# A hybrid decoder layer: gates and branch projections with tokens on partitions, the merged sum transposed for the output projection

## The chip, the cores and the metric

The kernel runs on one core of one Trainium2 chip. The metric is the time of one execution on the device, in microseconds (us). The engines: TensorE (PE in the rows, PEld its weight loads), VectorE (DVE), ScalarE (ACT), GpSimd (POOL), and SyncE (SP), which here only issues DMAs.

## The reference, cut to what matters

One layer on x of 256 tokens by 1024 channels, float32:

```
h = RMSNorm(x);  P = h @ w_in            # columns: rwkv 1792, attention 1536, pool 512, gates 3 x 1024
y0 = RWKV-7 time mixing (8 heads x 64), y1 = causal attention with ALiBi (8 x 64), y2 = pooling (4 x 128)
branch[n] = y[n] @ w_branch[n]           # 512 -> 1024 channels each, n = 0, 1, 2
x = x + (sum over n of sigmoid(P_gate[n]) * branch[n]) @ w_out
x = x + relu(RMSNorm(x) @ w_ff1)^2 @ w_ff2      # 1024 -> 4096 -> 1024
```

## The kernel before, in words

Every large product is done as three matmuls of rounded parts: a value is split into a high part and a remainder (w_hi and w_lo for weights, h_hi/h_lo, y_hi/y_lo, r_hi/r_lo for activations), and `mm3` (lines 460 to 463) adds high x high, high x low and low x high in one PSUM bank.

The weights pass through in 69 slots, the list `UNITS` (lines 59 to 69), 1 MB each, in two pieces of 128x1024. For each piece SyncE issues a DMA into `stage` (3 buffers, lines 433 to 436), ScalarE casts it to w_hi (line 823, "high") and VectorE subtracts to w_lo (line 1047, "low"), both into rings of 6 (`RING`). `split_places` sets the order: in slot t both engines prepare pieces 2t + 5 and 2t + 6. TensorE raises `used` after each half slot, and that frees ring places.

A slot has four quarters, p = 0 to 3; `part(t, p)` issues its dense matmuls, and `extra(t, p)` after it the small work of the mixers that is laid between. TensorE, ScalarE and VectorE walk the same (t, p) in program order: in a slot, ScalarE and VectorE do the first piece, extra 0, the second piece, extra 1, extra 2, `finish(t)` (what drains the slot's own result), extra 3.

The slots: 0 to 10 rwkv and attention columns, 11 and 12 the attention values, 13 and 14 pool columns, 15 to 26 the gates (`S_GATE` = 15), 27 to 32 the branches n = 1, 2, 0, each in two channel halves (`S_BR` = 27), 33 to 36 the output projection (`S_OUT` = 33), 37 to 68 the MLP.

There are two forms of a slot. In "feat" (and the branches before), 128x128 blocks of the weights are the stationary operand and the 256 tokens move: 48 matmuls of 256 columns, result with channels on partitions. In "tok" (slots 11 and 12, the output projection, and the second MLP product), a 128-token block of the activations is stationary and 512 weight columns move: 24 matmuls of 512 columns, result with tokens on partitions. A tok product of 1024 channels deep takes two slots for one 128x512 result per token half tt.

PSUM has 8 banks. `plan_turns` (lines 108 to 145) gives each result a bank; names without a fixed bank take 4 to 7 in turn (the ring), in the order in which TensorE comes to them. `room` makes TensorE wait until all earlier results of that bank are drained; `take` makes a reader wait until a result is there; `copied` waits for its drain. Before the change, feat slots use banks 0 and 1 in turn, attention scores bank 2, the transposed probabilities "pt" and the products "pv" bank 3, branches 0/1 and 2/3 in turn.

The mixers around the change: attention heads 0 to 7 run over slots 13 to 21 (score and pt after quarter 1, pv after quarter 3); the second half of the RWKV chunk work starts with "prod" (1, g, kind, e) over slots 17 and 18, which VectorE masks and copies (lines 1153 to 1165), goes on over slots 19 to 24, and ends with apply and group norm in 25 to 28.

Gates: ScalarE writes tanh(x/2) of each gate slot to `gates` (line 993). Branches: VectorE computes (tanh + 1) x branch (line 1298), GpSimd adds branches 1 and 2 (line 1428), VectorE adds branch 0 (line 1305), ScalarE writes y_hi = 0.5 x sum (line 999) and VectorE y_lo (line 1309). This sum has channels on partitions, as the output projection needs it for its stationary operand; TensorE waits there for `m_ready`.

## Time and profile before

| | us |
|---|---|
| median of 3 runs | 511.68 (510.59 to 511.97) |
| the profiled execution, whole | 510.58 |
| its span, first to last instruction | 508.8 |
| VectorE busy in it | 308.6 |
| ScalarE busy in it | 242.7 |
| GpSimd busy in it | 45.6 |

The mean granted clock of TensorE is 0.999. The span is what the timeline's microseconds count in; it starts at 0. Busy times of engines overlap, so they don't add up to it. The page's TensorE rows give each matmul from its start to its modelled end, and consecutive ones overlap: what one costs in a dense stretch is read from start to start.

### The profile page before, as it was taken

The page shows a single profiled execution, that of the slowest core. Times are in us where ns is not written, and L with a number is a line of the kernel's source. Part 1 is how long each engine was busy: PE and PEld are TensorE (multiplying, and loading weights), DVE is VectorE, ACT ScalarE, POOL GpSimd, SP SyncE. Part 2 cuts the span into 40 slices and gives each one's busy share as a digit, 9 for nine tenths or more (in the row PEclk, how much of TensorE's full clock was granted, in tenths as well). Part 3 has the DMA queues.
Part 4 walks back from the last instruction along what each step waited for, and adds up shares of the span by engine and source line. Part 5 has one row for each costly group of instructions (what it writes and reads, how often), then busy time and mean ns, then how long its engine had stood idle before and what let it go on. Part 6 is the DMA issues. An engine that isn't in the chain of part 4 may idle for free.

```text
span 508.8 us, 9618 instructions
## 1 busy us (share of the span) xinstructions
PE 494.9 (97%) x4064; PEld 451.0 (89%) x4064; DVE 308.6 (61%) x447; ACT 242.7 (48%) x365; POOL 45.6 (9%) x48
## 2 busy tenths in 40 slices
PE   3999999999999989999999999999999999999997
PEld 3989998988889778899999998899999999999995
DVE  4656898744463897446427986676555655555542
ACT  5676552454653236555333335655444544545440
POOL 1002003220660120000001220000000000000000
PEclk9999999999999999999999999999999999999999
DMA  9975462444422213454225557367666665665612
GB/s 262 270 210 160 133 172 78 126 124 125 126 84 83 84 55 112 126 140 131 84 84 170 177 166 194 124 203 222 195 183 191 187 186 173 200 197 180 200 44 82
DMA packets 101660, 76.87 MB, mean 151 GB/s; under 512 B 2545, under 2 KB 93297, under 8 KB 101618
## 3 DMA queue, kind: packets, MB, share of 16 engines
q1 hardware_dynamic: 101618, 76.26, 50.6%
q8 instruction: 32, 0.52, 0.4%
q14 instruction: 10, 0.08, 0.1%
HBM read 75.20 MB, written 1.05 MB: 150 GB/s over the span
## 4 chain that ended last, share of the span: by engine, by line
PE 93%; DVE 4%; ACT 1%; DMA 1%; issue 1%; POOL 0%; ACTq 0%; POOLq 0%
PE bank L461 26%; PE bank L462 25%; PE bank L463 25%; PE bank L691 1%; PE bank L669 1%; PE bank L707 1%; PE bank L554 1%; DMA xs<-in_x 1%; PE bank L785 1%; DVE mat L1157 1%; PE bank L742 1%; PE bank L731 1%; PE bank L741 1%; PE bank L723 1%; PE bank L635 1%
## 5 line engine op out<-in xcount | busy, mean ns | idle before, releaser
L1047 DVE TENSOR_TENSOR w_lo<-stage,w_hi 128x1024 fp32r<-128x1024 f32 x138 | 171.6, 1249 | 121.1 <-ACT w_hi L823 121.0
L823 ACT CAST w_hi<-stage 128x1024 fp32r<-128x1024 f32 x138 | 143.7, 1048 | 117.8 <-PE bank L463 90.4
L461 PE MATMUL bank<-h_hi,w_hi 128*128 128x256 f32 x656 | 193.0, 294 | 0.9 <-DVE h_lo L1071 0.7
L462 PE MATMUL bank<-h_lo,w_hi 128*128 128x256 f32 x656 | 186.4, 284 | 0.0
L463 PE MATMUL bank<-h_hi,w_lo 128*128 128x256 f32 x656 | 186.2, 284 | 0.0
L461 PEld LDWEIGHTS bank<-h_hi,w_hi 128*128 128x128 f32 x656 | 126.3, 193 | 9.7 <-issue 6.8
L462 PEld LDWEIGHTS bank<-h_lo,w_hi 128*128 128x128 f32 x656 | 126.6, 193 | 0.6
L463 PEld LDWEIGHTS bank<-h_hi,w_lo 128*128 128x128 f32 x656 | 126.4, 193 | 0.0
L461 PE MATMUL bank<-w_hi,r_hi 128*128 128x512 f32 x128 | 50.0, 391 | 0.0
L462 PE MATMUL bank<-w_lo,r_hi 128*128 128x512 f32 x128 | 50.0, 390 | 0.0
L463 PE MATMUL bank<-w_hi,r_lo 128*128 128x512 f32 x128 | 49.8, 389 | 0.0
L1363 POOL TENSOR_TENSOR small<-small 128x8 f32<-128x8 f32 (+2 forms) x9 | 14.1, 1568 | 170.4 <-DVE small L1215 104.7
L463 PEld LDWEIGHTS bank<-w_hi,r_lo 128*128 128x128 f32 x128 | 24.0, 188 | 5.1
L461 PEld LDWEIGHTS bank<-w_hi,r_hi 128*128 128x128 f32 x128 | 24.1, 188 | 4.6
L462 PEld LDWEIGHTS bank<-w_lo,r_hi 128*128 128x128 f32 x128 | 24.1, 188 | 4.4
L1012 ACT ACTIVATE mat<-bank 128x512 f32<-128x512 f32 x16 | 9.6, 598 | 28.0 <-PE bank L463 27.9
L1321 DVE TENSOR_TENSOR mat<-mat 128x512 f32<-128x512 f32 x16 | 11.1, 691 | 19.2 <-ACT mat L1012 19.2
L461 PE MATMUL bank<-y_hi,w_hi 128*128 128x256 f32 x64 | 18.2, 284 | 0.0
L463 PE MATMUL bank<-y_hi,w_lo 128*128 128x256 f32 x64 | 18.1, 283 | 0.0
L462 PE MATMUL bank<-y_lo,w_hi 128*128 128x256 f32 x64 | 18.1, 283 | 0.0
L940 ACT ACTIVATE att<-att,small 128x128 f32<-128x128 f32 (+1 forms) x16 | 7.2, 448 | 21.4 <-DVE small L1246 21.4
L461 PE MATMUL bank<-w_hi,y_hi 128*128 128x512 f32 x32 | 12.5, 392 | 0.0
(210 smaller groups left out, 613.7 us busy)
## 6 DMA issues: line engine op xcount, KB each, us to landing
stage<-in_w_ff SPq DMA_DIRECT2D x64, 512.0 KB, 4.3
stage<-in_w_in SPq DMA_DIRECT2D x54, 512.0 KB, 3.9
stage<-in_w_branch SPq DMA_DIRECT2D x12, 512.0 KB, 3.6
stage<-in_w_out SPq DMA_DIRECT2D x8, 512.0 KB, 3.4
xs<-in_x SPq DMA_DIRECT2D x2, 512.0 KB, 4.4
out<-xs SPq DMA_DIRECT2D x4, 256.0 KB, 2.1
cst<-in_consts SPq DMA_DIRECT2D x1, 897.0 KB, 7.4
lora<-in_g_up SPq DMA_DIRECT2D x1, 256.0 KB
```

The costliest lines, as they stand in the source:

```text
L461: pe.matmul(o, lh, rh, start=first, stop=False)
L462: pe.matmul(o, lh, rl, start=False, stop=False)
L463: return pe.matmul(o, ll, rh, start=False, stop=last)
L554: ins = pe.matmul(o[:, 256 * i:256 * i + 256], bk[c][rows, kind, j], ar[c][rows, j], start=True, stop=True)
L635: ins = pe.matmul(o[:, 4 * c + 2 * jj:4 * c + 2 * jj + 2], sq_att[n % 2][:, T * jj + P * c:T * jj + P * c + P], cst[:, C_BLK:C_BLK + P:HD] ...
L669: ins = pe.matmul(both[b][to, HD * j:HD * j + HD], gm[rows, 2 * j + e, 0, rows], x_c[rows, 2 * j + e], start=True, stop=True)
L823: nc.scalar.copy(w_hi[:, v % RING], stage[:, v % STAGES]).then_inc(hi_done, 1)
L940: nc.scalar.activation(w, w, ACT.Exp, bias=nmax[:, tt:tt + 1], accum_out=psm[:, tt:tt + 1]).then_inc(exps_ready, 1)
L1012: nc.scalar.activation(ffs[i % 2], o[:], ACT.Relu).then_inc(drained_of(("ff", i)), 1)
L1047: dve.tensor_tensor(w_lo[:, v % RING], stage[:, v % STAGES], w_hi[:, v % RING].bitcast(F32), ALU.subtract)\
L1321: link(dve.tensor_tensor(fsq[i % 2], ffs[i % 2], ffs[i % 2], ALU.mult))
L1363: pool.tensor_tensor(ap, ap, half.to_broadcast(shape), ALU.pow).then_inc(done, 1)
```

## The change

The gates become tok slots: six groups of 512 columns, each two slots (depth halves) long, in banks (2g + tt) mod 3; the tanh of both token halves comes at the end of the second slot. The branch slots become tok slots too, half a depth per piece, tokens on partitions; VectorE's multiply-add and addition go by token half. Scores move to bank 3; pt, pv and the pool products move into the ring of banks 4 to 7. The merged sum now has tokens on partitions and goes through four groups of four transposes ("mt", `turned_place`) in slots 32 and 33; ScalarE and VectorE write y_hi and y_lo from their PSUM result. The arithmetic is the same.

```diff
@@ -60,7 +60,8 @@
 UNITS += [("feat", N_RWKV + N_ATTN + c) for c in (0, 256)]
-UNITS += [("feat", N_RWKV + N_ATTN + N_POOL + 256 * q) for q in range(12)]
+GATES_AT = N_RWKV + N_ATTN + N_POOL
+UNITS += [("tok", GATES_AT + 512 * g, kh) for g in range(6) for kh in range(2)]
@@ -125,12 +126,16 @@
                     use(("unit", t), t % 2, dense=True)
+                elif u[0] == "tok" and u[2] == 0 and u[1] >= GATES_AT:
+                    g = (u[1] - GATES_AT) // 512
+                    for tt in range(TT):
+                        use(("tok", u[1], tt), (2 * g + tt) % 3, dense=tt == 1)
...
                     b = 2 * ((t - S_BR + 1) % 2)
-                    use(("unit", t, 0), b, dense=True)
+                    use(("unit", t, 0), b)
@@ -143,6 +148,11 @@
     return turn
+
+
+def turned_place(t, p):
+
+    return {(S_OUT - 1, 1): (0, 0), (S_OUT - 1, 2): (0, 1), (S_OUT, 1): (1, 0), (S_OUT, 3): (1, 1)}.get((t, p))
@@ -197,13 +207,15 @@
         if p == 1 and h >= 1:
-            out += [(("pt", h - 1), 3)]
+            out += [(("pt", h - 1),)]
         if p == 1 and h < HEADS:
-            out += [(("score", h), 2)]
+            out += [(("score", h), 3)]
         if p == 3 and h >= 1:
-            out += [(("pv", h - 1), 3)]
+            out += [(("pv", h - 1),)]
     if t == S_PY and p in (0, 2):
-        out += [(("pool", p // 2), 2 + p // 2)]
+        out += [(("pool", p // 2),)]
+    if turned_place(t, p):
+        out += [(("mt", *turned_place(t, p)),)]
@@ -216,8 +228,8 @@
         for tt in range(TT):
-            if u[0] == "branch":
-                ends[("unit", t, tt)] = 2 * t + 1 + tt
+            if u[0] == "branch" and tt == 1:
+                ends[("unit", t, 1)] = 2 * t + 2
@@ -385,7 +397,7 @@
         pad_ready, pool_step, pd_ready, yp_hi = (sem(n) for n in ("pad_ready", "pool_step", "pd_ready", "yp_hi"))
@@ -394,7 +406,7 @@
             kind = UNITS[v // 2][0]
-            k = {"feat": KD, "ff1": KD, "ff2": 1, "branch": W // P}.get(kind, 2)
+            k = {"feat": KD, "ff1": KD, "ff2": 1}.get(kind, 2)
@@ -408,9 +420,8 @@
             if u[0] == "branch":
-                c = 512 * u[2] + 256 * half
-                return w_branch[0, u[1], :, c:c + 256].rearrange("(k p) n -> p k n", p=P)
-            if u[0] == "tok":
+                r, m, c = 256 * half, w_branch[0, u[1]], 512 * u[2]
+            elif u[0] == "tok":
@@ -503,12 +514,15 @@
                             pe.wait_ge(yr_ready, TT)
-                    rh, rl, k0 = {1: (y_hi, y_lo, 0), 2: (y_hi, y_lo, 4), 0: (r_hi, r_lo, 0)}[u[1]]
-                    name = ("unit", t, p // 2)
-                    o = ps(name) if i else room(pe, name)
-                    for k in range(W // P):
-                        ins = mm3(o[:, T * i:T * i + T], wh[:, k, P * i:P * i + P], wl[:, k, P * i:P * i + P],
-                                  rh[:, k0 + k], rl[:, k0 + k], k == 0, k == W // P - 1)
+                    lh, ll, k0 = {1: (y_hi, y_lo, 0), 2: (y_hi, y_lo, 4), 0: (r_hi, r_lo, 0)}[u[1]]
+                    name = ("unit", t, i)
+                    o = room(pe, name) if p < 2 else ps(name)
+                    for kk in range(2):
+                        k = 2 * (p // 2) + kk
+                        ins = mm3(o[:], lh[:, k0 + k, P * i:P * i + P], ll[:, k0 + k, P * i:P * i + P],
+                                  wh[:, kk], wl[:, kk], k == 0, k == 3)
+                    if p == 2:
+                        ins.then_inc(full_of(name), 1)
@@ -516,8 +530,8 @@
                         first, last = u[1] == 0, u[1] == 1
-                        if i == 0:
-                            pe.wait_ge(m_ready, 2 * u[1] + p // 2 + 1)
+                        if p < 2:
+                            copied(pe, ("mt", u[1], i))
@@ -795,6 +809,13 @@
                     ins.then_inc(full_of(("pool", i)), 1)
+                if turned_place(t, p):
+                    ch, tt = turned_place(t, p)
+                    pe.wait_ge(m_pre, 2 * ch + tt + 1)
+                    o = room(pe, ("mt", ch, tt))
+                    for k in range(4):
+                        ins = pe.transpose(o[:, P * k:P * k + P], gates[ch][:, tt, P * k:P * k + P], ident)
+                    ins.then_inc(full_of(("mt", ch, tt)), 1)
@@ -951,6 +972,11 @@
                     ins.then_inc(yp_hi, 1)
+                if turned_place(t, p):
+                    ch, tt = turned_place(t, p)
+                    o = take(act, ("mt", ch, tt))
+                    nc.scalar.mul(y_hi[:, 4 * ch:4 * ch + 4, P * tt:P * tt + P], o[:].rearrange("p (k t) -> p k t", k=4), 0.5)\
+                      .then_inc(m_hi, 1)
@@ -983,21 +1009,18 @@
                     nc.scalar.activation(sq_att[n % 2], o[:], ACT.Square).then_inc(drained_of(("unit", t)), 1)
+                elif S_GATE <= t < S_BR:
+                    if u[2] == 1:
+                        for tt in range(TT):
+                            name = ("tok", u[1], tt)
+                            o = take(act, name)
+                            nc.scalar.activation(gates[(t - S_GATE) // 2][:, tt], o[:], ACT.Tanh, scale=0.5)\
+                              .then_inc(drained_of(name), 1)
...
                         nc.scalar.copy(vatt[:, tt], o[:]).then_inc(drained_of(name), 1)
-                elif S_GATE <= t < S_BR:
-                    o = take(act, ("unit", t))
-                    nc.scalar.activation(gates[(t - S_GATE) // 2][:, t % 2 ^ S_GATE % 2], o[:], ACT.Tanh, scale=0.5)\
-                      .then_inc(drained_of(("unit", t)), 1)
-                elif u[0] == "branch" and u[1] == 0:
-                    for i in range(2):
-                        m = 2 * u[2] + i
-                        act.wait_ge(m_pre, m + 1)
-                        nc.scalar.mul(y_hi[:, 2 * m:2 * m + 2], gates[u[2]][:, i].rearrange("p (k t) -> p k t", k=2), 0.5)\
-                          .then_inc(m_hi, 1)
@@ -1265,6 +1288,14 @@
                     ins.then_inc(drained_of(("pool", i)), 1)
+                if turned_place(t, p):
+                    ch, tt = turned_place(t, p)
+                    dve.wait_ge(m_hi, 2 * ch + tt + 1)
+                    o = take(dve, ("mt", ch, tt))
+                    part = y_hi[:, 4 * ch:4 * ch + 4, P * tt:P * tt + P].bitcast(F32)
+                    dve.scalar_tensor_tensor(out=y_lo[:, 4 * ch:4 * ch + 4, P * tt:P * tt + P], in1=part, scalar=0.5,
+                                             in0=o[:].rearrange("p (k t) -> p k t", k=4), op0=ALU.mult, op1=ALU.subtract)\
+                       .then_inc(drained_of(("mt", ch, tt)), 1)
@@ -1292,23 +1323,16 @@
                     g = 2 * n + ch
-                    for i in range(2):
-                        copied(dve, ("unit", S_GATE + 2 * g + i))
-                        o = take(dve, ("unit", t, i))
-                        dve.scalar_tensor_tensor(out=gates[g][:, i], in0=gates[g][:, i], scalar=1.0, in1=o[:],
+                    for tt in range(TT):
+                        copied(dve, ("tok", GATES_AT + 512 * g, tt))
+                        o = take(dve, ("unit", t, tt))
+                        dve.scalar_tensor_tensor(out=gates[g][:, tt], in0=gates[g][:, tt], scalar=1.0, in1=o[:],
                                                  op0=ALU.add, op1=ALU.mult)\
-                           .then_inc(drained_of(("unit", t, i)), 1)
-                    if n == 0:
-                        dve.wait_ge(sum_ready, ch + 1)
-                        for i in range(2):
-                            copied(dve, ("unit", t, i))
-                            dve.tensor_tensor(gates[ch][:, i], gates[ch][:, i], gates[2 + ch][:, i], ALU.add).then_inc(m_pre, 1)
-                        for i in range(2):
-                            m = 2 * ch + i
-                            dve.wait_ge(m_hi, m + 1)
-                            dve.scalar_tensor_tensor(out=y_lo[:, 2 * m:2 * m + 2], scalar=0.5, op0=ALU.mult, op1=ALU.subtract,
-                                                     in0=gates[ch][:, i].rearrange("p (k t) -> p k t", k=2),
-                                                     in1=y_hi[:, 2 * m:2 * m + 2].bitcast(F32)).then_inc(m_ready, 1)
+                           .then_inc(drained_of(("unit", t, tt)), 1)
+                        if n == 0:
+                            dve.wait_ge(sum_ready, ch + 1)
+                            copied(dve, ("unit", t, tt))
+                            dve.tensor_tensor(gates[ch][:, tt], gates[ch][:, tt], gates[2 + ch][:, tt], ALU.add).then_inc(m_pre, 1)
```

## Rows read from the trace of the kernel before

**Rows 1.** The page: busy time of each engine, and the engines of the chain.

```profile
PE 494.9 (97%) x4064; PEld 451.0 (89%) x4064; DVE 308.6 (61%) x447; ACT 242.7 (48%) x365; POOL 45.6 (9%) x48
...
PE 93%; DVE 4%; ACT 1%; DMA 1%; issue 1%; POOL 0%; ACTq 0%; POOLq 0%
```

**Rows 2.** Windows, slots 27 to 32: length, then PE, PEld, DVE, ACT, POOL busy, clock, DMA, GB/s.

```profile
266.20:301.20 35.00, 35.00 (x294) 35.00 (x294) 29.17 (x36) 14.80 (x17) 7.79 (x3) 1.00 0.54 167
```

**Rows 3.** Timeline of PE, slot 18: start, us, engine, line, out<-in, count [idle before <-releaser].

```profile
185.24 0.52 PE L769 MATMUL bank<-cst,att 128*128 128x128 f32 x3 [2.00 <-DVE y_lo L1051]
```

**Rows 4.** Timeline of PE: first matmul of slots 27, 28, 33 and 34.

```profile
266.16 0.28 PE L461 MATMUL bank<-y_hi,w_hi 128*128 128x256 f32 x1
...
271.92 0.28 PE L461 MATMUL bank<-y_hi,w_hi 128*128 128x256 f32 x1
...
301.15 0.40 PE L461 MATMUL bank<-w_hi,y_hi 128*128 128x512 f32 x1
...
306.62 0.39 PE L461 MATMUL bank<-w_hi,y_hi 128*128 128x512 f32 x1
```

**Rows 5.** Timeline of POOL, ACT and DVE, slot 31 and the start of slot 32.

```profile
291.97 3.23 POOL L1428 TENSOR_TENSOR big<-big 128x1024 f32<-128x1024 f32 x1 [2.45 <-DVE big L1298]
...
292.76 1.05 ACT L823 CAST w_hi<-stage 128x1024 fp32r<-128x1024 f32 x1 [1.83 <-PE bank L463]
...
293.85 2.44 DVE L1047 TENSOR_TENSOR w_lo<-stage,w_hi 128x1024 fp32r<-128x1024 f32 x1 [0.91 <-ACT w_hi L823]
296.21 1.27 DVE L1298 SCALAR_TENSOR_TENSOR big<-big,bank 128x512 f32<-128x512 f32 x2
297.41 1.28 DVE L1305 TENSOR_TENSOR big<-big 128x512 f32<-128x512 f32 x2
```

**Rows 6.** Timeline of PE: first quarter of slots 10 and 11, and what follows it.

```profile
94.01 0.36 PE L461 MATMUL bank<-h_hi,w_hi 128*128 128x256 f32 x1
...
95.61 0.50 PE L669 MATMUL bank<-mat 64*64 64x64 f32 x17
...
102.71 0.47 PE L461 MATMUL bank<-w_hi,h_hi 128*128 128x512 f32 x1
...
104.27 0.69 PE L669 MATMUL bank<-mat 64*64 64x64 f32 x32
```

**Rows 7.** Timeline of PE, slot 12: four transposes and the two matmuls after them.

```profile
115.71 0.60 PE L645 MATMUL bank<-cst,att 128*128 128x128 f32 x4
116.06 0.48 PE L461 MATMUL bank<-w_hi,h_hi 128*128 128x512 f32 x1
116.38 0.39 PE L462 MATMUL bank<-w_lo,h_hi 128*128 128x512 f32 x1
```

**Rows 8.** Timeline of DVE, slots 17 and 18.

```profile
181.80 0.67 DVE L1157 TENSOR_TENSOR mat<-bank,cst 128x512 f32<-128x512 f32 x1
...
185.12 1.23 DVE L1047 TENSOR_TENSOR w_lo<-stage,w_hi 128x1024 fp32r<-128x1024 f32 x1
186.38 1.29 DVE L1157 TENSOR_TENSOR mat<-bank,cst 128x512 f32<-128x512 f32 x2
```

**Rows 9.** Timeline of ACT, slot 26.

```profile
260.60 0.60 ACT L993 ACTIVATE big<-bank 128x512 f32<-128x512 f32 x1 [0.85 <-PE bank L463]
...
264.95 0.63 ACT L926 ACTIVATE lmix<-lora 128x512 f32<-128x512 f32 x1 [2.82 <-DVE lora L1211]
265.49 1.03 ACT L823 CAST w_hi<-stage 128x1024 fp32r<-128x1024 f32 x1
266.43 0.59 ACT L993 ACTIVATE big<-bank 128x512 f32<-128x512 f32 x1
```

**Rows 10.** Timeline of ACT and PE, end of slot 14 and start of slot 15.

```profile
137.93 0.59 ACT L1005 COPY ops<-bank 128x512 f32<-128x512 f32 x1
...
138.57 0.39 PE L461 MATMUL bank<-h_hi,w_hi 128*128 128x256 f32 x1
```

More of the change, by code:

```diff
@@ L387, in build_layer @@
         pad_ready, pool_step, pd_ready, yp_hi = (sem(n) for n in ("pad_ready", "pool_step", "pd_ready", "yp_hi"))
-        sum_ready, m_pre, m_hi, m_ready = (sem(n) for n in ("sum_ready", "m_pre", "m_hi", "m_ready"))
+        sum_ready, m_pre, m_hi = (sem(n) for n in ("sum_ready", "m_pre", "m_hi"))
         ss2_ready, h2_hi = sem("ss2_ready"), sem("h2_hi")
```

## The prediction

> **What bounds the kernel now.** I read the chain of work that ended last first: 93% of it is TensorE, which is busy for 97% of the span [rows 1]. The reader is to see that a microsecond off TensorE's queue is a microsecond off the span, and that any new wait of TensorE is one on. Then the windows. In the branch stage (slots 27 to 32, 266.2 to 301.2 us) TensorE is busy for all 35.0 us, VectorE for 29.2 and ScalarE for 14.8, with DMA at 0.54 [rows 2], so VectorE is second, with little to spare. The one wait of TensorE inside the changed stages is the 2.0 us at 185.24, for VectorE [rows 3]. Each slot brings 1 MB of weights in both forms, cast and subtracted two to three slots ahead: the w_lo instruction at 293.85 makes the first piece of slot 34, which TensorE touches at 306.62 [rows 4, 5]. Supply is therefore not what I look at. The question is the order of TensorE's queue and its banks.
>
> **The gain: half as many matmuls, each twice as wide.** A slot in the old form is 48 matmuls of 256 columns, in the new form 24 of 512. The columns streamed are the same. With nothing between, a slot of 48 takes 271.92 - 266.16 = 5.76 us (0.120 each) and a slot of 24 takes 306.62 - 301.15 = 5.47 us (0.228 each) [rows 4]; that slot's first quarter is slower because it follows 256-wide work, the others take 1.36 us, so a bare quarter (p = 0 to 3) goes from 1.44 to 1.36: 0.08 us saved. Where other matmuls stand around a quarter, less is left: with the same neighbours before and after, the 256-wide quarter takes 95.61 - 94.01 = 1.60 us and the 512-wide one 104.27 - 102.71 = 1.56 [rows 6]: 0.04 saved.
> I count quarters by what the code puts before them. Slots 15 and 16: 8 with neighbours, 0.32 us. Slots 17 and the first half of 18: 6, which earn nothing, since TensorE then waits for VectorE anyway [rows 3]. From there to slot 25: 24 with neighbours and 6 bare, 0.96 + 0.48 = 1.44. Slots 26 to 32: 28 bare, 2.24, less 0.04 at the two re-entries. Together 0.32 + 1.44 + 2.20 = 4.0 us. Ends: 3.0 (0.05 in every bare quarter, if the slower pitch stays) and 4.8 (0.08 in every quarter that counts, with slots 17 and 18).
>
> The Trainium skill, TensorE: Matmul & The Clock Gate, section Back-to-back issue gap, gives the gap between isolated matmuls as N/2.4 + 2.5 ns, a fixed part of 2.5 ns where the rows above hold some 13 ns at either width. By that page of the Trainium skill, an estimate, the 432 matmuls that go would bring 432 x 2.5 ns = 1.1 us and the sum below would be 2.9 us worse. The rows are of this very form in this kernel, so they decide.
>
> **The transposes.** The merged sum now has tokens on partitions and must be turned: 16 transposes of 128x128 f32 in four groups, at (slot 32, after p = 1 and p = 2) and (slot 33, after p = 1 and p = 3), all in TensorE's queue. The same shape in groups of four stands between 512-wide quarters in slot 12: 116.06 - 115.71 = 0.35 us, and the first matmul after it takes 0.32 instead of 0.23 [rows 7]. With the slower pitch of the quarter behind (0.03) that is 0.46 a group, 1.85 us for four. Ends 1.4 (without re-entry) and 2.2. ScalarE's four multiplications and VectorE's four subtractions for y_hi and y_lo were there before at the same size (128x512), now read from PSUM; they cost nothing by themselves, since neither engine is the bound, but they move in their queues, which is a term below.
>
> **New wait 1: the shared ring (slot 18).** The gates take banks 0 to 2, so pt and pv go from bank 3 into the ring of banks 4 to 7. Following the uses: pt of head 4, after p = 1 of slot 18, gets the bank of product (1,1,kind 1,e 0), issued after p = 0 of that slot. VectorE is a phase behind there: it drains the kind-0 products at 181.80, then the pv remainder, then a w_lo at 185.12, and only then the kind-1 products from 186.38, the first of two done at about 187.0 [rows 8]. Before, pt waited only for the pv remainder and went at 185.24 [rows 3]. Now it goes at about 187.15: 1.9 us on. Two earlier waits of the ring (some 0.8 us for product (1,0,kind 2,e 1), 0.6 us for (1,1,kind 1,e 1)) and the last kind-2 product's wait for pv fall inside this one. Behind pt in the queue stand score 5, the rest of slot 18 and everything after; VectorE needs score 5 only after the pair at 186.38 and one more w_lo (188.8), so it isn't pushed on and the loss isn't doubled. Ends: 0 (the old wait only) and 2.5 (both kind-1 products drained first). I take 1.9, straight from the row.
>
> **New wait 2: bank 2 at slot 27.** Branch unit (27, tt 0) takes bank 2, whose last user is the second token half of gate 5; it is complete only when slot 26 ends. TensorE reaches slot 27 at 260.39 + 5.44 = 265.83 in old time (slot 26 started one slot before 266.16, less its 0.08 a quarter) and must wait for the tanh. ScalarE's order there is tanh, w_hi, square, w_hi, tanh [rows 9]. The first tanh (slot 25) goes, since only every second gate slot drains now, so w_hi, the group norm's chain through VectorE and the square come 0.5 earlier; the w_hi of 265.49 starts at about 265.0, the two tanh follow at 265.95 and 266.45 and end at 267.05. TensorE starts at 267.15: 1.3 us. Ends 0.6 (one tanh after the slot's end) and 1.9 (nothing moves up: the two from 266.43). Before, the bank of the next slot was always free a slot earlier.
>
> **Other banks.** Gate 0 takes bank 0 at slot 15, that of unit 14: its copy runs 137.93 to 138.52 and TensorE arrives at 138.57 [rows 10], so it costs 0 to 0.2; I take 0. In the other gates the third bank gives a quarter and the extras as cover, about 1.5 us against one 0.6 us tanh that can start a quarter before the slot's end: 0, at worst 0.5.
>
> **New wait 3: VectorE between the merge and the output projection.** In slot 31 VectorE ends its second w_lo late, at 296.3, because of the GpSimd addition beside it; the two multiply-adds and two additions then run to 298.7 [rows 5]. In old time the new slot 31 starts 0.2 earlier; the first transposes wait until the first addition (297.4) and TensorE comes at 297.6, so 0 there. But VectorE then has two w_lo (to 301.0) before the first y_lo of the transposed block, done at 301.65, and the output projection (slot 33) is reached at 301.2: 0.5 us, with the semaphore. The second block's y_lo (302.3) is before its use (303.2). Slot 34 and later have a slot's room. Ends 0 and 1.9 (one more w_lo plus its wait ahead of it).
>
> **The sum.** -4.0 + 1.85 + 1.9 + 1.3 + 0.5 = +1.55, taken as +1.6 us. The MLP (slots 37 on) isn't touched and keeps its pace. The profiled execution took 510.6 us, of which 508.8 are its span; so 510.4 span and 512.2 for a profiled execution. The median of the runs shown, 511.68, is 1.1 above the profiled one; the difference is put on the median: 513.3 us. 0.3%, here 1.5 us, is about what can be told from no change; the forecast lies at that edge.
>
> **Rivals.**
> Faster. The covers hold after all: pt's and bank 2's waits are short, because VectorE and ScalarE run ahead once TensorE pauses. For it: in slots 19 to 26 TensorE never waits. Against: both waits follow from instructions that stand in program order with rows for each. Price: -4.0 + 1.85 = -2.15, so 509.5; it decides below 510.1, where at most 0.6 of the three waits may be left. 12%.
> Much slower. VectorE becomes the bound around slots 28 to 36: 29.2 of 35.0 us busy already [rows 2], slots shorter by 0.3 each, and a chain addition, transposes, w_lo, y_lo at the projection's start. If each of the four transposed blocks is met one w_lo (1.23) late, not one block 0.5 late, +4.4 more at most, about +2.5 likely: 515.8. Against: the w_lo run far ahead. 15%.
> The 512-wide form gives less than in the MLP: the pitch of 0.232 of slots 11 and 12 and of the first quarter of slot 33 stays. Gain 3.0 instead of 4.0: 514.3. By the gap that the Trainium skill states there the same mechanism, pushed to its end, gives 516.2. 13%, nearly all of it on the former, as [rows 4] speak against it.
> The forecast, with its own spread of about 1 us: 60%.
>
> **How the numbers follow.** Slower by over 0.3% (above 513.2): half of the forecast's 60, most of the third and all of the second rival: 0.53. Faster (below 510.1): 0.10. Same: 0.37. Range 511.0 to 515.8: below it most of the first rival, above it the tail of the second; about 2 in 10.
>
> **What would show it.** On TensorE: 18 slots of 24 wide matmuls, a bare one of 5.44 to 5.47 us; groups of four transposes at 0.35; idle before pt (head 4) of about 3 to 4 us in all over slots 17 and 18, where it was 2.0, released by the kind-1 product's copy; about 1.3 idle ahead of slot 27 released by the tanh; half a microsecond ahead of slot 33 released by y_lo. If the waits are there and the span still falls, the wide quarters gave more than 0.08 and 0.04. If TensorE waits in slots 28 to 36 for w_lo or y_lo beyond 1 us, the second rival holds.

## The result, and the profile after

The changed kernel takes 515.20 us, the median of four runs (514.51 to 515.66); the kernel before took 511.83 beside it (510.59 to 512.04). The ratio is 1.0076, with a 95% interval of 1.0056 to 1.0096: slower, inside the range forecast, and 1.9 us above the 513.3 that was forecast. The change itself costs 3.4 us, where 1.6 were forecast. The profiled execution took 515.11 us, 513.3 of them its span, with a mean granted clock of TensorE of 0.993; before, it was 510.58, 508.8 and 0.999.

The page of the changed kernel: TensorE still bounds it, with 416 fewer matmuls (432 go, 16 transposes come), yet more busy time than in [rows 1]. The row of PEclk, the granted clock in 40 slices, has a 7 in it.

```profile
PE 498.4 (97%) x3648; PEld 429.9 (84%) x3648; DVE 309.3 (60%) x447; ACT 242.6 (47%) x365; POOL 45.6 (9%) x48
...
PEclk9999999999999979999999999999999999999999
...
PE 91%; DVE 5%; ACT 1%; DMA 1%; issue 1%; SPq 0%; ACTq 0%
```

The longest waits of TensorE (line waited at, releaser: us in total, times, longest). The first is the start of the kernel. Then come pt of head 4 (L783) for the copy of a product, the branch stage for the tanh (L1017), and products (L571) for a copy; the 0.4 put down to "issue" is the one at slot 33.

```profile
PE bank L553 <- DVE big L1082: 6.9, 1, 6.9
PE bank L783 <- DVE mat L1180: 1.4, 1, 1.4
PE bank L472 <- ACT big L1017: 1.2, 1, 1.2
PE bank L472 <- DVE h_lo L1094: 0.7, 1, 0.7
PE bank L571 <- DVE mat L1180: 0.5, 1, 0.5
PE bank L472 <- issue: 0.4, 1, 0.4
```

The timeline of TensorE through slots 17 and 18, with lines left out between. Two waits stand in brackets. Two more hide in the durations: the eight matmuls at 179.80 take 2.00 us, where eight of the same kind take 1.14 at 176.34, and the eight at 183.33 take 1.49, where they took 0.72 to 0.79 in the kernel before. Together 0.54 + 0.86 + 0.75 + 1.36 = 3.5 us without work. Behind it a wide matmul starts every 0.43 us (191.16 to 191.58), and no longer every 0.23.

```profile
174.12 0.71 PE L571 MATMUL bank<-ops 64*128 64x128 f32 x4 [0.54 <-DVE mat L1180]
176.34 1.14 PE L568 MATMUL bank<-ops 64*128 64x256 f32 x8
...
179.80 2.00 PE L568 MATMUL bank<-ops 64*128 64x256 f32 x8
183.33 1.49 PE L571 MATMUL bank<-ops 64*128 64x128 f32 x8
186.18 0.74 PE L783 MATMUL bank<-cst,att 128*128 128x128 f32 x3 [1.36 <-DVE mat L1180]
...
191.16 0.63 PE L472 MATMUL bank<-w_hi,h_hi 128*128 128x512 f32 x1
191.58 0.63 PE L473 MATMUL bank<-w_lo,h_hi 128*128 128x512 f32 x1
```

The windows say why (columns as in [rows 2]; the column before the last two is the granted clock). From 186.1 to 193.0 TensorE is busy and its clock is 0.52, its lower level of 1.2 GHz; just behind, it is 1.00 again.

```profile
186.10:193.00 6.90, 6.82 (x18) 4.91 (x19) 5.66 (x16) 2.06 (x6) 1.09 (x1) 0.52 0.52 152
193.20:196.20 3.00, 3.00 (x28) 1.77 (x29) 0.81 (x2) 1.91 (x3) 0.00 (x0) 1.00 0.00 0
```

The price, piece by piece against the same pieces at 2.4 GHz (in the kernel of experiment 1 below): pt, the score and the way to the next quarter take 2.25 us instead of 1.30, and the two quarters behind, each with what follows it, 2.73 and 2.40 instead of 1.49 and 1.46; together 3.1 us. The forecast had no such term.

The timeline of TensorE at slot 27, in the branch stage, at a group of transposes and at slot 33: a wait of 1.20 for the tanh, bare wide matmuls whose w_hi step is 0.68 us (twice that, 1.36, is a quarter), and a wait of 0.45.

```profile
269.90 0.47 PE L472 MATMUL bank<-w_hi,y_hi 128*128 128x512 f32 x1 [1.20 <-ACT big L1017]
...
276.14 0.39 PE L472 MATMUL bank<-w_hi,y_hi 128*128 128x512 f32 x1
276.82 0.39 PE L472 MATMUL bank<-w_hi,y_hi 128*128 128x512 f32 x1
...
300.41 0.60 PE L817 MATMUL bank<-cst,big 128*128 128x128 f32 x4
300.77 0.48 PE L472 MATMUL bank<-w_hi,r_hi 128*128 128x512 f32 x1
...
304.67 0.47 PE L472 MATMUL bank<-w_hi,y_hi 128*128 128x512 f32 x1 [0.45 <-issue]
```

Laid on each other at the first weight matmul, the traces differ so, in us: wide form -3.8; slot 0, which the change doesn't touch, -0.2; waits of slots 17 and 18 +2.0; lower clock behind them +3.1; slot 27 +1.36; transposes, slot 33 and gate 0's bank +2.6. That is +5.1. The first weight matmul came 0.5 earlier after the change (11.25 against 11.79), by nothing that it does, which leaves the +4.5 of the spans.

### The profile page after: what moved, and what is told of

The parts are those of the page before. It is cut to its first block, busy times and chain, and to the rows that moved or that the text cites. A ratio compares the mean times of both kernels' runs of the same rounds, so it can differ in the third digit from the quotient of the medians.

```text
span 513.3 us, 8782 instructions
## 1 busy us (share of the span) xinstructions
PE 498.4 (97%) x3648; PEld 429.9 (84%) x3648; DVE 309.3 (60%) x447; ACT 242.6 (47%) x365; POOL 45.6 (9%) x48
## 4 chain that ended last, share of the span: by engine, by line
PE 91%; DVE 5%; ACT 1%; DMA 1%; issue 1%; SPq 0%; ACTq 0%
PE bank L472 26%; PE bank L474 24%; PE bank L473 24%; PE bank L705 1%; PE bank L683 1%; PE bank L721 1%; DMA stage<-in_w_in 1%; PE bank L568 1%; DVE mat L1180 1%; ACT w_hi L844 1%; DVE w_lo L1070 1%; PE bank L799 1%; PE bank L756 1%; PE bank L745 1%; PE bank L790 1%
## 5 line engine op out<-in xcount | busy, mean ns | idle before, releaser
L472 PE MATMUL bank<-h_hi,w_hi 128*128 128x256 f32 x464 | 135.0, 291 | 0.9 <-DVE h_lo L1094 0.7
L473 PE MATMUL bank<-h_lo,w_hi 128*128 128x256 f32 x464 | 132.3, 285 | 0.0
L474 PE MATMUL bank<-h_hi,w_lo 128*128 128x256 f32 x464 | 132.2, 285 | 0.0
L472 PEld LDWEIGHTS bank<-h_hi,w_hi 128*128 128x128 f32 x464 | 89.8, 194 | 5.0 <-issue 3.4
L473 PEld LDWEIGHTS bank<-h_lo,w_hi 128*128 128x128 f32 x464 | 89.9, 194 | 0.6
L474 PEld LDWEIGHTS bank<-h_hi,w_lo 128*128 128x128 f32 x464 | 89.8, 194 | 0.0
L472 PE MATMUL bank<-w_hi,h_hi 128*128 128x512 f32 x112 | 49.7, 443 | 0.0
L474 PE MATMUL bank<-w_hi,h_lo 128*128 128x512 f32 x112 | 44.8, 400 | 0.0
L473 PE MATMUL bank<-w_lo,h_hi 128*128 128x512 f32 x112 | 44.7, 400 | 0.0
L474 PE MATMUL bank<-w_hi,y_lo 128*128 128x512 f32 x64 | 25.0, 391 | 0.0
## 6 DMA issues: line engine op xcount, KB each, us to landing
stage<-in_w_ff SPq DMA_DIRECT2D x64, 512.0 KB, 4.1
stage<-in_w_in SPq DMA_DIRECT2D x54, 512.0 KB, 3.9
stage<-in_w_branch SPq DMA_DIRECT2D x12, 512.0 KB, 3.9
stage<-in_w_out SPq DMA_DIRECT2D x8, 512.0 KB, 4.6
xs<-in_x SPq DMA_DIRECT2D x2, 512.0 KB, 3.9
```

The costliest lines, as they stand in the source:

```text
L472: pe.matmul(o, lh, rh, start=first, stop=False)
L473: pe.matmul(o, lh, rl, start=False, stop=False)
L474: return pe.matmul(o, ll, rh, start=False, stop=last)
```

## The experiments

The kernel before ran beside each batch, on the same chip: 511.61 us (33 runs, 510.05 to 512.63) beside the first four, 511.45 (29 runs, 510.34 to 512.58) beside the next four, 511.53 (30 runs, 510.37 to 512.93) beside the last four. The ratios below are against these, with 95% intervals.

### 1. Work put into the idle time of slot 18

Theory: the idle time in slots 17 and 18 let the clock fall. So it is filled, with eight matmuls into bank 3 that nobody reads.

```diff
+                if (t, p) == (18, 1):
+                    o = room(pe, ("score", 5))
+                    for _ in range(8):
+                        pe.matmul(o[:], h_hi[:, 0, 0:P], h_hi[:, 0:2].rearrange("p k t -> p (k t)"), start=True, stop=True)
```

> The changed kernel, with eight extra 512-column matmuls of h_hi into bank 3 (the scores' bank, overwritten by score 5) after quarter 1 of slot 18, ahead of the kind-2 products: about 1.8 us of work in time in which TensorE otherwise waits for bank 5 and then for bank 6. Theory (the granted clock falls to half because TensorE was idle in slots 17 and 18): the clock stays full, pt of head 4 still starts when the kind-1 product is drained, and the kernel gains the 3.0 us that half speed costs: about 512.2 us. Rival (the wide form or chance lowers the clock there): the clock falls as before, 515.2 us, up to 515.7 if the extra matmuls push pt.

512.0 us (510.75 to 513.49), ratio 1.001 (0.9999 to 1.0022): eight matmuls more, and 3.2 us less than the changed kernel. Timeline and window of this kernel, the same stretch:

```profile
183.01 1.98 PE L665 MATMUL bank<-h_hi 128*128 128x512 f32 x8
184.92 0.72 PE L571 MATMUL bank<-ops 64*128 64x128 f32 x8
185.96 0.52 PE L787 MATMUL bank<-cst,att 128*128 128x128 f32 x3 [0.32 <-DVE mat L1184]
```

```profile
186.10:193.00 6.90, 6.90 (x53) 4.75 (x56) 5.87 (x17) 3.54 (x9) 1.09 (x1) 1.00 0.50 152
```

pt starts when it did, because VectorE is what it waits for (185.96, and 186.18 in the changed kernel), but what follows goes at full clock: 53 matmuls in the window, small ones among them, where there were 18. In all 12 runs the mean clock was 1.00. Without the idle time the clock didn't fall. In the traces the price is 3.1 us; by the medians it is 3.2 us, or 2.8 against the changed kernel's runs of experiment 12.

### 2. Slot 27's banks swapped

```diff
-                    b = 2 * ((t - S_BR + 1) % 2)
+                    b = 2 * ((t - S_BR) % 2)
...
-                        use(("out", u[2], tt), 2 * (1 - u[2]) + tt, dense=tt == 1)
+                        use(("out", u[2], tt), 2 * u[2] + tt, dense=tt == 1)
```

> The changed kernel with the branches' bank pairs swapped (slot 27 takes banks 0 and 1, slot 32 banks 2 and 3, the output projection's halves swapped to match). Theory (bank 2 alone makes TensorE wait at slot 27): no wait there, 1.3 us less, 513.9 us. Rival (TensorE meets a tanh anyway, at quarter 1 of slot 27 or at slot 28): less than 0.3 us gained, 515.0 or more.

514.58 us (511.42 to 514.79), ratio 1.0048 (1.0033 to 1.0064). The wait of slot 27 is gone, and TensorE stands 1.38 us at the first transposes instead. (The profiled execution had a mean clock of 0.997: the same waits in slots 17 and 18, but a stretch at half clock of only 3.4 us behind them.) Timeline of TensorE and of VectorE in this kernel:

```profile
298.48 0.66 PE L817 MATMUL bank<-cst,big 128*128 128x128 f32 x4 [1.38 <-DVE big L1335]
```

```profile
291.27 1.27 DVE L1329 SCALAR_TENSOR_TENSOR big<-big,bank 128x512 f32<-128x512 f32 x2
292.47 4.55 DVE L1070 TENSOR_TENSOR w_lo<-stage,w_hi 128x1024 fp32r<-128x1024 f32 x2
296.95 0.67 DVE L1329 SCALAR_TENSOR_TENSOR big<-big,bank 128x512 f32<-128x512 f32 x1
297.73 0.69 DVE L1335 TENSOR_TENSOR big<-big 128x512 f32<-128x512 f32 x1
```

VectorE's additions stand behind two w_lo that take 4.55 us together; a w_lo with nothing beside it takes 1.23 [rows 8], and from 292.71 to 295.93 GpSimd runs its addition. (By the Trainium skill, SBUF — State Buffer, section Who interferes with whom, a VectorE instruction with two SBUF inputs contends with a GpSimd instruction that reads SBUF; these rows agree.) So the gain was given back 30 us later, by neither of the two accounts: VectorE has no more room there than slot 27's wait had given it.

### 3. The kernel before, with the ring alone

Only the banks of pt, scores, pv and pool are changed, as the change has them; the 256-wide form stays.

```diff
-            out += [(("pt", h - 1), 3)]
+            out += [(("pt", h - 1),)]
...
-            out += [(("score", h), 2)]
+            out += [(("score", h), 3)]
...
-            out += [(("pv", h - 1), 3)]
+            out += [(("pv", h - 1),)]
...
-        out += [(("pool", p // 2), 2 + p // 2)]
+        out += [(("pool", p // 2),)]
```

> The kernel before, with one part of the change alone: scores in bank 3, pt, pv and the pool products in the ring of banks 4 to 7. Gates and branches keep their 256-column form, nothing is transposed. Theory (the shared ring brings the wait, and the idle time brings the lower clock): pt of head 4 starts 1.9 us later, and the clock falls to half for some 7 us, 3.0 us more: about 4.9 us over the kernel before. Rival (the wide form is needed for the fall): 1.9 us over the kernel before and the clock full.

512.84 us, ratio 1.0036 (1.0015 to 1.0057). The 12 runs spread over 510.84 to 515.69. Every run comes with its mean granted clock, and that sorts them: 1.00 in five (510.84 to 511.99, mean 511.4), 0.997 in two (512.8 and 512.9), 0.993 in five (513.90 to 515.69, mean 515.0). One program, and its groups lie 3.6 us apart. The profiled execution, 515.14 us, was one of the last group; its wait and its window are those of the changed kernel:

```profile
186.89 0.87 PE L769 MATMUL bank<-cst,att 128*128 128x128 f32 x3 [1.36 <-DVE mat L1157]
```

```profile
186.50:193.30 6.80, 6.41 (x26) 5.46 (x27) 5.98 (x17) 1.47 (x5) 1.09 (x1) 0.51 0.56 157
```

The fall needs no wide matmul. The ring alone brings it, but not in each execution, and so the median is neither the theory's +4.9 us nor the rival's +1.9. Whether an execution with clock 1.00 also waited less could not be seen, since one of the 12 was profiled; that the ring's own +1.7 to +2.0 us is missing from the mean of the five at 1.00 (511.4) speaks for it.

### 4. Gates in two banks, pt and pv kept in bank 3

```diff
-                        use(("tok", u[1], tt), (2 * g + tt) % 3, dense=tt == 1)
+                        use(("tok", u[1], tt), 1 - tt, dense=tt == 1)
...
...
-            out += [(("pt", h - 1),)]
+            out += [(("pt", h - 1), 3)]
-            out += [(("score", h), 3)]
+            out += [(("score", h), 2)]
-            out += [(("pv", h - 1),)]
+            out += [(("pv", h - 1), 3)]
...
-        out += [(("pool", p // 2),)]
+        out += [(("pool", p // 2), 2 + p // 2)]
```

> The changed kernel with the banks of before for everything but the gates: gates in banks 1 (first token half) and 0, scores in 2, pt and pv in 3, pool products in 2 and 3; so the next branch slot's bank 2 is free too. Theory: the ring's wait (1.9), the half clock (3.0) and the wait at slot 27 (1.3) all go, and two banks are enough for the gates since the first half's tanh starts a quarter before the slot's end: 6.2 us less than the changed kernel, about 509.0 us, faster than the kernel before by 1.5 to 3 us. Rival (two banks are too few: each of the five gate changes waits for a tanh, 0.5 to 0.8 us each): 512 us.

512.91 us (511.92 to 514.63), ratio 1.0033 (1.002 to 1.0045). That is 3.9 us over the theory's 509.0. pt's wait is back to the 2.00 of [rows 3], slot 27's is gone, but 1.02 us of waiting stand at the first transposes, as in experiment 2; the clock kept 1.00 in the profile. A new wait stands in slot 19. Timeline of TensorE, then of ScalarE:

```profile
192.08 0.47 PE L472 MATMUL bank<-w_hi,h_hi 128*128 128x512 f32 x1 [2.46 <-ACT big L1017]
```

```profile
190.47 0.40 ACT L961 ACTIVATE att<-att,small 128x128 f32<-128x128 f32 x1 [4.92 <-DVE small L1269]
...
191.37 1.06 ACT L1017 ACTIVATE big<-bank 128x512 f32<-128x512 f32 x2
```

The tanh that frees the bank stands behind the exponentials, and these wait 4.92 us for VectorE. The rival had small waits at every gate; it is one large one. The third bank is what hides the tanh there.

### 5 and 6. VectorE's split moved behind the products, without and with the swap

```diff
+                both = t in (17, 18)
-                for v in split_places(2 * t):
+                for v in () if both else split_places(2 * t):
...
-                for v in () if late else split_places(2 * t + 1):
+                for v in () if late or both else split_places(2 * t + 1):
...
-                for v in split_places(2 * t + 1) if late else ():
+                for v in (*split_places(2 * t), *split_places(2 * t + 1)) if both else split_places(2 * t + 1) if late else ():
```

> The changed kernel, where VectorE does its w_lo of slots 17 and 18 after extra 3 of the slot instead of between (same instructions, pieces needed two slots later). Theory (TensorE's waits in slots 17 and 18 stand behind VectorE's four w_lo there, 1.2 us each, one of them with a wait for w_hi; the half clock comes from those waits): the waits of the ring and also the wait of 2.0 us that the kernel before had go, the clock stays full; left over the kernel before are -4.2 (wide form) - 2.0 + 1.85 (transposes) + 1.35 (slot 27) + 0.6 (projection) = -2.4: about 509.2 us. Rival (VectorE's chain of products and softmax itself is too long): the waits of TensorE there are still over 2 us in all, 511 us or more.

> The kernel with deferred w_lo, and also the branches' bank pairs swapped, so that slot 27 doesn't wait for the tanh in bank 2. Theory (what slot 27 no longer waits, the transposes in slot 32 wait for VectorE's merge instead, as in the run with the swap alone): within 0.4 us of the run with the deferral alone. Rival (the wait at slot 32 came from the disturbed slot 18): 1.3 us less than it.

511.52 us (510.49 to 513.36), ratio 1.0003 (0.9989 to 1.0016), and with the swap 512.37 (510.88 to 512.98), ratio 1.001 (0.9997 to 1.0023). The first is 2.3 us over the theory's 509.2, and the rival's waits of over 2 us are there: pt still waits, now 2.50 us in one piece, because slot 17's own two w_lo (2.36 us) still stand ahead of the products:

```profile
181.92 2.36 DVE L1070 TENSOR_TENSOR w_lo<-stage,w_hi 128x1024 fp32r<-128x1024 f32 x2
184.31 1.29 DVE L1180 TENSOR_TENSOR mat<-bank,cst 128x512 f32<-128x512 f32 x2
```

But the scattered waits ahead of it are gone, and in this trace so is the fall behind it; the median is 3.7 us less than the changed kernel's for 1 us less of waiting. None of its 12 runs had a mean clock of 0.993. That isn't the whole story, though: the sixth kernel has the same code in slots 17 and 18 and the same single wait, and in its profiled execution the clock fell behind it. The wait and the window of the sixth, then the window of the fifth:

```profile
183.51 0.52 PE L783 MATMUL bank<-cst,att 128*128 128x128 f32 x3 [2.50 <-DVE mat L1180]
```

```profile
183.50:190.40 6.90, 6.89 (x19) 4.95 (x19) 4.45 (x15) 3.11 (x7) 1.09 (x1) 0.54 0.36 133
```

```profile
185.10:192.00 6.90, 6.85 (x41) 4.71 (x45) 5.78 (x17) 4.71 (x10) 1.10 (x1) 1.00 0.38 138
```

So one wait of 2.50 us can be followed by the fall, and four pieces aren't needed for it. What the deferral changed, in these runs, is how often it comes: a mean clock of 0.993 or less in 5 of the 36 runs of the fifth, sixth and seventh, against 8 of the 11 of the changed kernel (here and in experiment 12). The swap again took 1.35 off slot 27 and gave 1.4 to the transposes, as its theory had it.

### 7. The swap, with VectorE's late w_lo moved too

On top of the sixth: in slots 31 to 33 the second w_lo (and in 32 and 33 the second w_hi) goes behind the merge.

```diff
-                late = t == S_FF - 1
+                late = t in (S_OUT - 2, S_OUT - 1, S_OUT, S_FF - 1)
```

> As the run with deferral and swapped banks, and VectorE also does the second w_lo of slots 31, 32 and 33 after extra 3 (ScalarE the second w_hi of 32 and 33). Theory (the merge comes late because a w_lo, blocked by the GpSimd addition, stands ahead of it in slot 31, and two stand ahead of the first y_lo): TensorE's waits in slots 32 and 33 go, 1.9 us less than the run with deferral alone: about 507.3 us, faster than the kernel before by some 4 us. Rival (w_lo arrive too late for the slots after, or the merge waits for the branch result itself): 509 us or more.

510.10 us (508.34 to 514.01), ratio 0.9979 (0.9958 to 1.0001). The waits at slots 27, 32 and 33 are gone together: with room on VectorE the swap pays. It is 1.4 us less than the fifth, where 1.9 were expected, and 2.8 over the theory's 507.3, most of which is what the fifth was over its own. Its profiled execution also had half the clock behind pt's wait of 2.50 us, from 183.9 to 190.7.

### 8. The kernel before, with the split moved

> The kernel before, with the same deferral of VectorE's w_lo in slots 17 and 18 and nothing of the change. Theory: its one wait in that stage (2.0 us) goes, 509.6 us. Rival (the wait moves to another instruction): 511 us or more.

509.67 us (508.60 to 509.89), ratio 0.9956 (0.9939 to 0.9972). The time is the theory's 509.6, but the rival's mechanism is there too: the 2.0 us of [rows 3] are gone, and 1.63 stand later for ScalarE's copy:

```profile
188.73 0.62 PE L785 MATMUL bank<-att,big 128*64 128x256 f32 x2 [1.63 <-ACT att L935]
```

The mean clock was 0.999 or 1.00 in five of its six runs, where the kernel before had 0.997 in 74 of the 92 runs beside all batches. Between the profiled executions the gain is 0.9 us (spans of 507.9 and 508.8), between the medians 1.8; what makes the rest was not found.

### 9 to 11. The split of three pieces held until after slot 18

In slots 17 and 18 VectorE splits nothing but the first piece of slot 17; the three others are held to the end of slot 18. Alone, with the swap and the late w_lo of the seventh, and in the kernel before:

```diff
-                for v in split_places(2 * t):
+                for v in () if t == 18 else split_places(2 * t):
...
-                for v in () if late else split_places(2 * t + 1):
+                for v in () if late or t in (17, 18) else split_places(2 * t + 1):
...
-                for v in split_places(2 * t + 1) if late else ():
+                for v in range(40, 43) if t == 18 else split_places(2 * t + 1) if late else ():
```

> The changed kernel, where VectorE holds three w_lo (pieces 40, 41, 42) until after extra 3 of slot 18. In the deferral run the two w_lo of slot 17 still stood ahead of the kind-1 products in slot 18, and a w_hi waited for its DMA; here nothing of the kind stands there. Theory: the kind-1 product is drained within 0.5 us of when TensorE comes for its bank, no wait over 0.7 us before pt of head 4, and the clock stays full in all runs: 2.3 us less than the deferral run, about 509.2 us. Rival (VectorE's own work on products, softmax and group norm is what TensorE waits for): a wait of 2 us or more stays, 511 us.

> Held w_lo as in the run before, swapped bank pairs for the branches, and the second w_lo of slots 31, 32 and 33 after extra 3 (w_hi of 32 and 33 too). Theory: all waits that the change brought are gone but the transposes' own time: before - 4.2 (wide form) - 2.0 (its old wait) + 1.9 (transposes) + 0.2 = 4.1 us under the kernel before, about 507.3 us. Rival (the lower clock comes with any wait over 1 us somewhere in slots 17 to 19): some runs at 510 us, median over 508.5.

> The kernel before with the same three w_lo held. Theory: its wait of 2.0 us goes and no other takes its place: 509.4 us, so that the run with all repairs is 2 us below it (wide form 4.2, transposes 1.9). Rival (the wide form gives nothing once waits are gone): the two are equal.

Alone 511.94 us (509.45 to 512.97), ratio 1.0002 (0.9985 to 1.0019): no wait ahead of pt, and 2.24 us in slot 19: the theory's 509.2 is missed, and the rival's 2 us of waiting are there, though not for its reason. Timeline of TensorE and VectorE:

```profile
196.81 0.69 PE L705 MATMUL bank<-mat 64*64 64x64 f32 x32 [2.24 <-DVE mat L1206]
```

```profile
188.75 3.48 DVE L1070 TENSOR_TENSOR w_lo<-stage,w_hi 128x1024 fp32r<-128x1024 f32 x3
194.71 1.22 DVE L1070 TENSOR_TENSOR w_lo<-stage,w_hi 128x1024 fp32r<-128x1024 f32 x1 [2.48 <-ACT w_hi L844]
195.85 0.75 DVE L1206 TENSOR_TENSOR mat<-bank,cst 128x256 f32<-128x256 f32 x2
```

The wait was moved by a slot, not taken away: the product's copy stands behind w_lo there too. With swap and late w_lo it is 509.93 (507.22 to 511.82), ratio 0.9965 (0.9948 to 0.9982): the one version of the changed kernel that beats the kernel before, by 0.35%. The theory's 507.3 was reached by the run of 507.22 alone; the rival (a median over 508.5, by the clock) came. The four runs at a mean clock of 0.999 or 1.00 took 508.0 in the mean, the eight others 510.3. In the kernel before the same hold gives 511.62 (509.56 to 513.93), ratio 0.9996 (0.9979 to 1.0014), and not the 509.4 expected: here too a wait takes the old one's place in slot 19, with 3.4 us at half clock behind it.

```profile
196.67 0.69 PE L691 MATMUL bank<-mat 64*64 64x64 f32 x32 [2.56 <-DVE mat L1183]
```

It lies 1.7 above the tenth, where 2 were expected; the five runs at 1.00 (mean 510.0) lie 2.0 above the tenth's four. With much the same wait left in both, that is what wide form and transposes are worth, -4.0 + 1.85 in the forecast. The eighth, the kernel before with the split moved, is no slower than the tenth by its ratio.

### 12. The changed kernel once more

> The changed kernel as it is, beside the others. Theory (the clock falls in most executions but not in all, by where the idle time of slots 17 and 18 falls): median 514.5 to 515.2 us, a spread of some 3 us, the fastest near 512 us, which is the sum without the clock's 3.0. Rival: all within 1 us.

514.76 us (512.97 to 515.59), ratio 1.0053 (1.0033 to 1.0073). Five of the seven runs had a mean clock of 0.993 (mean 515.0 us); the two others, 0.997 and 1.00, took 513.0. Median and spread are the theory's; the fastest lie 1 us above its 512, so that the clock is worth 2.0 us between these groups.

## Why the prediction was right in direction and in the terms that it had, and 1.9 us low

Wide form, -4.0: measured -3.8. A bare quarter went from 1.44 to 1.36 us, one with neighbours lost some 0.04; from the start of slot 27 to that of slot 32 it is 1.4 us (27.79 against 29.23). The rows of slots 11, 12 and 33 carried over to the stages that took the form.

Transposes, +1.85: a group costs 0.36 to 0.38 and some 0.1 at the re-entry, as [rows 7] gave it.

Shared ring, +1.9: +2.0, which is how much longer pt starts after VectorE's copy of the kind-0 products (5.44 us, where it was 3.44). The 3 to 4 us of idle time over the two slots were 3.5.

Bank 2 at slot 27, +1.3: +1.36 from start to start, 1.20 of it shown as idle, released by the tanh. The order that the prediction gave ScalarE (w_hi, then both tanh) is the order of the trace:

```profile
267.75 1.03 ACT L844 CAST w_hi<-stage 128x1024 fp32r<-128x1024 f32 x1
268.69 1.07 ACT L1017 ACTIVATE big<-bank 128x512 f32<-128x512 f32 x2
```

Slot 33, +0.5: 0.45 shown idle, about 0.6 with the slower first matmul, right after y_lo; its two w_lo stood ahead as told:

```profile
301.61 2.36 DVE L1070 TENSOR_TENSOR w_lo<-stage,w_hi 128x1024 fp32r<-128x1024 f32 x2
303.88 1.28 DVE L1296 SCALAR_TENSOR_TENSOR y_lo<-bank,y_hi 128x512 fp32r<-128x512 f32 x2
```

Gate 0's bank, 0: 0.1. VectorE as the bound (the second rival) did not come; this window answers to [rows 2], with TensorE busy for 34.35 of 34.80 us (the 0.45 of slot 33 are missing), and VectorE at 84% of it:

```profile
270.40:305.20 34.80, 34.35 (x157) 28.07 (x156) 29.18 (x37) 14.39 (x16) 7.76 (x3) 1.00 0.57 175
```

What the prediction lacked stands in its first step: "any new wait of TensorE is one on". A wait can also decide at which clock the work behind it runs. pt's wait was priced at its length; the idle time of 3.5 us around it cost 3.1 us more behind it in the profiled execution. In the trace that makes the sum +1.55 + 3.1 = +4.7, against a span longer by 4.5. No rival held this: all three were about order and pitch, and the covers were judged at one clock. [rows 2] shows a clock of 1.00 and the text passed over it, since in that window nothing waits.

That only 1.9 us were missing in the end is luck. By its own sum the profiled execution should have taken 512.2 us; it took 515.1, 2.9 more. The prediction then added 1.1 us, because the kernel before had its median that far above its profiled execution. After the change that distance was 0.1 (515.11 and 515.20), so 1.0 of the 2.9 us were covered by a term that had nothing to do with them.

Why the kernel before had that distance stays open. The mean clock doesn't explain it: of its 92 later runs the six at 1.00 (mean 511.2) and the 74 at 0.997 (511.3) are alike, and only the eleven at 0.993 (512.5) are slower. In which slot its clock falls was not profiled.

## What to carry to other kernels

Where TensorE is the bound, price each of its waits twice: by its length, and by the clock of the work behind it. The second price comes only in a share of the executions, so take it from several runs and not from one profile. Count the waits that hide in long durations too. Compare the mean clock of the runs before reading a difference of under one per cent, and look into a profile for where the clock fell: the mean doesn't say it. Two waits on one second engine are one debt: freeing TensorE at slot 27 was paid at slot 32 until VectorE itself had less ahead of the merge.

## What was not expected of the hardware

The granted clock fell to half for 6.8 us after four pieces of idle time, none over 1.4 us, 3.5 us in all between 174 and 186. After one piece of 2.0 in the same place (the profiled kernel before), after one of 2.5 (the fifth) and after 2.24 us in slot 19 (the ninth) it stayed at 1.00. But after one piece of 2.5 in the sixth and in the seventh it fell for 6.8 us, too, and 2.56 us in the eleventh and 2.17 us in the tenth, both in slot 19, were followed by a stretch at half of some 3.4 us. The tenth:

```profile
196.00:200.00 4.00, 4.00 (x40) 2.76 (x41) 2.52 (x6) 1.97 (x8) 0.00 (x0) 0.57 0.76 200
```

So the same wait can have it or not, and runs of one program differ by 2 to 3.6 us with it. The share of runs with a mean clock of 0.993 or less goes roughly with the idle time: 8 of 11 in the changed kernel and 6 of 10 with the swap alone, 5 of 12 with the ring alone, 5 of 36 with the deferral, 11 of 92 in the kernel before, none of 12 with the idle time filled. The Trainium skill, TensorE: Matmul & The Clock Gate, section What's actually happening, has the array throttled by default and freed by activity, with two levels; the two levels agree with the 0.52 and 1.00 above. What decides when an execution falls is left open here.

Not each fall costs time. In the profiled execution of the fifth the mean clock of 0.996 comes from slot 0, long before anything that was changed, where the clock was at half from 13.5 to 17.0 us. Slot 1 began at 19.71 us there, and at 19.80 in the kernel before, where the row says 1.00. But in that kernel, too, the 256-wide matmuls from 12.14 to 16.62 us start every 0.21 us, and every 0.12 behind: it ran at half pace with a granted clock of 1.00 in the row. Windows of the fifth and of the kernel before:

```profile
14.00:17.00 3.00, 3.00 (x16) 3.00 (x16) 2.38 (x4) 1.04 (x1) 0.00 (x0) 0.50 1.03 355
```

```profile
14.00:17.00 3.00, 3.00 (x17) 3.00 (x16) 2.27 (x2) 0.81 (x1) 0.00 (x0) 1.00 1.07 319
```

So a mean of 0.997 in one kernel and 1.00 in another need not be time lost, and the pitch of the matmuls is the surer witness.
